# Attention's preparation: a stage of its own, or turned products and a side program within the first projection

## The chip, the cores and the metric

The kernel runs on one core of a Trainium2 chip. The time is that of the device in microseconds; lower is better. All data is float32 in memory.

## The reference

A chain of three layers over 1,024 latent and 256 context tokens of width 1,024: an attention layer, a recurrent layer (RWKV scan and a long convolution), and a block with gated mixing, a forgetting attention and a feed-forward net. The change concerns the first layer's input projection and what stands between it and the attentions:

```python
u = modulate(x, norm_g, shift, scale) @ w_in            # 1,280 tokens, 3,328 columns
qa, ka, va, ga, qb, kb, vb, gb = split_cols(u, (512, 512, 512, 512, 512, 128, 128, 512))
# local attention: qa (scaled), ka as they are
# grouped attention: 8 query and 2 key heads of 64
q_lat = apply_axial_rope(rms_norm(to_heads(qb, 8), q_gain), cos, sin)
k_lat = apply_axial_rope(rms_norm(to_heads(kb, 2), k_gain), cos, sin)
```

## The kernel before

The program is a sequence of stages. Each opens its own tiles and semaphores (`Stage`), writes one program for each engine, and ends by clearing its semaphores behind a barrier of all engines. Nothing is reordered: every engine runs its instructions as they are written, and semaphores order them against each other. All transfers named below are issued by SP.

`front_stage` makes the modulated tokens, turned, as a high and a low part (`xT`). `gemm_stage`, here named g1, then multiplies them with the weights: blocks of 416 columns, ten token tiles m of 128 in each block, eight steps k of 128, and three matmuls a step (high x high, high x low, low x high), so 24 matmuls for one product of 128 tokens and 416 columns. Each block of weights is loaded once (`w`) and split into a high part `wh` by ScalarE and a low part `wl` by VectorE, in four groups; both exist twice, so the next block's are made while this one's are used. There is a ring of five accumulators (`acc`) and five output tiles (`o`); VectorE evacuates even tiles m, ScalarE odd ones, and SP stores them into U1. VectorE's part of a split stands behind its second evacuation (m = 2), ScalarE's behind its second (m = 3). The sixth projection (named g6, 6 blocks of 428 columns, eight tiles) is a stage of the same kind.

`attn_prep_stage` follows g1. It reads U1 back and loops over five pairs of token tiles. For each pair, local attention's queries and keys (columns 0 to 1,023) are turned on TensorE (L508) and evacuated by ScalarE (L498), the queries scaled. The ten grouped heads (columns 2,048 to 2,687) are squared (ScalarE, L492), summed (VectorE, L523), a root taken (ScalarE, L494), scaled by its reciprocal and the gain (L526 to L529), rotated (L534 to L539), turned (TensorE, L514) and evacuated (VectorE). SP stores the 13 turned blocks into QT and waits for that store before the next pair. Ahead of the loop the stage zeroes three rows of U2. `na_stage` (local attention) and `gqa_stage` (grouped attention) read QT and U1.

The line on which the steps around a split rest, in VectorE's program of g1:

```python
for g in range(G):
    dve.wait_ge(high_out, (j * 2 + b) * G + g + 1)
    low(dve, wl[b][:, ks, :], w[:, ks, :], wh[b][:, ks, :]).then_inc(low_out, 1)
```

## Time and profile before

| | us |
|---|---|
| median of three runs | 5,387.6 |
| the runs | 5,382.7 to 5,405.49 |
| the profiled execution's own time | 5,381.02 |
| its span | 5,379.2 |
| mean granted TensorE clock | 0.895 |

The span runs from the first to the last instruction of one execution, which the hardware profiler recorded; start times count from its beginning. PE is TensorE's matmuls, PEld its weight loads, DVE VectorE, ACT ScalarE, POOL GpSimd, SP the queue that issues transfers. PEclk is the share of its full speed (2.4 GHz) that TensorE's clock was granted. In a timeline, what stands in brackets is how long the engine had been idle and what released it; rows merge instructions of one line (xcount), and a matmul's length there is its passage, longer than the spacing of one to the next.

### The profile page before, as it was taken

To read this page: it belongs to the slowest core of one execution; us is meant where nothing else is said; L and a number is where in the kernel's file an instruction comes from. 1 tells how busy PE (TensorE), PEld (TensorE's weight loads), DVE (VectorE), ACT (ScalarE), POOL (GpSimd) and SP (SyncE) were. 2 spreads that over 40 slices of the span, in tenths; PEclk is the share of its full clock that TensorE was granted. 3 is DMA by queue.
4 is the path that set the end of the run, shared out by engine and by line. 5 is a ranking of instruction groups with operands and counts; after the bars stand their busy time and mean duration, and the time that the engine had idled before them with its cause. 6 is when DMAs were issued, how large, how long until landed. Compare 5 with 4: busy or idle time off the path is not lost. (4 is left out here: it accounts for less than half of the span.)

```text
span 5379.2 us, 67544 instructions
## 1 busy us (share of the span) xinstructions
PE 4458.7 (83%) x25392; PEld 3788.9 (70%) x25392; DVE 2287.8 (43%) x4035; ACT 1508.8 (28%) x3230; POOL 889.5 (17%) x844
## 2 busy tenths in 40 slices
PE   8998279797888942899999968996793946899998
PEld 2898178797788931899999933445793735688876
DVE  3111467334511236667776754465311534211134
ACT  2110145465411124222222223004211534221133
POOL 0000053100000753444444432000000000000000
PEclk9999589898999976899998978998896967899999
DMA  7222352202322665211111141114222213111121
GB/s 281 89 84 69 119 111 51 55 16 77 114 88 100 222 217 209 71 37 36 45 44 30 31 133 47 74 39 150 83 86 75 57 56 110 63 47 50 35 86 67
DMA packets 295432, 464.36 MB, mean 86 GB/s; under 512 B 76576, under 2 KB 215936, under 8 KB 290629
## 3 DMA queue, kind: packets, MB, share of 16 engines
q1 hardware_dynamic: 294894, 455.99, 26.5%
q10 hardware_dynamic: 288, 5.07, 0.3%
q8 instruction: 152, 2.49, 0.2%
q14 instruction: 98, 0.80, 0.0%
HBM read 336.97 MB, written 129.01 MB: 87 GB/s over the span
## 5 line engine op out<-in xcount | busy, mean ns | idle before, releaser
L372 PE MATMUL g_acc<-g_wh,l_x_high 128*128 128x416 f32 (+2 forms) x1856 | 636.3, 343 | 58.0 <-DVE g_wl L53 58.0
L372 PE MATMUL g_acc<-g_wh,l_x_low 128*128 128x416 f32 (+2 forms) x1856 | 638.0, 344 | 0.0
L372 PE MATMUL g_acc<-g_wl,l_x_high 128*128 128x416 f32 (+2 forms) x1856 | 634.5, 342 | 0.0
L1480 POOL TENSOR_TENSOR scan_X<-scan_GA,scan_masks 64x256 f32<-64x256 f32 x480 | 361.9, 754 | 241.5 <-ACT scan_GA L1408 206.9
L372 PEld LDWEIGHTS g_acc<-g_wh,l_x_high 128*128 128x128 f32 x1856 | 351.7, 189 | 64.6 <-DVE g_wl L53 60.6
L428 DVE COPY g_o<-g_acc 128x416 f32<-128x416 f32 (+2 forms) x116 | 65.5, 565 | 715.3 <-PE g_acc L372 715.3
L372 PEld LDWEIGHTS g_acc<-g_wl,l_x_high 128*128 128x128 f32 x1856 | 352.2, 190 | 5.9
L3051 POOL TENSOR_TENSOR g_x<-g_x,g_o 128x512 f32<-128x512 f32 x8 | 11.1, 1396 | 2082.3 <-ACT g_o L2989 2082.2
L372 PEld LDWEIGHTS g_acc<-g_wh,l_x_low 128*128 128x128 f32 x1856 | 351.5, 189 | 3.6
L415 ACT COPY g_o<-g_acc 128x416 f32<-128x416 f32 (+2 forms) x116 | 56.5, 487 | 880.4 <-PE g_acc L372 880.4
L2835 PE MATMUL ffi_acc<-l4a_x_high,ffi_wh 128*128 128x512 f32 x704 | 274.7, 390 | 13.4 <-DVE ffi_wl L53 13.4
L2835 PE MATMUL ffi_acc<-l4a_x_low,ffi_wh 128*128 128x512 f32 x704 | 274.4, 390 | 0.0
L2835 PE MATMUL ffi_acc<-l4a_x_high,ffi_wl 128*128 128x512 f32 x704 | 274.3, 390 | 0.0
L1278 PE MATMUL scan_bank<-scan_T,scan_X 128*128 128x64 f32 x1600 | 211.0, 282 | 20.5 <-DVEq L1589 12.2
L53 DVE TENSOR_TENSOR ffi_wl<-ffi_w,ffi_wh 128x1024 fp32r<-128x1024 f32 x44 | 53.9, 1225 | 392.5 <-ACT ffi_wh L2845 392.5
L1278 PEld LDWEIGHTS scan_bank<-scan_T,scan_X 128*128 128x128 f32 x1600 | 196.1, 197 | 28.0 <-POOL scan_X L1480 26.6
L1286 PE MATMUL scan_bank<-scan_Pm,scan_TT 128*128 128x64 f32 x1600 | 201.9, 281 | 0.0
L1286 PEld LDWEIGHTS scan_bank<-scan_Pm,scan_TT 128*128 128x128 f32 x1600 | 194.7, 199 | 0.0
L1416 ACT COPY scan_Pm<-scan_bank 128x256 f32<-128x256 f32 x200 | 74.5, 373 | 392.1 <-PE scan_bank L1278 392.1
L1695 POOL TENSOR_TENSOR g_cu<-g_cu,g_ctaps 128x1536 f32<-128x1536 f32 x24 | 85.5, 3562 | 555.0 <-DMA g_cu<-s_U 555.0
L53 DVE TENSOR_TENSOR g_wl<-g_w,g_wh 128x832 fp32r<-128x832 f32 (+2 forms) x104 | 106.4, 1085 | 155.0 <-ACT g_wh L412 155.0
L2835 PEld LDWEIGHTS ffi_acc<-l4a_x_high,ffi_wh 128*128 128x128 f32 x704 | 132.5, 188 | 41.2 <-issue 13.7
(476 smaller groups left out, 9929.3 us busy)
## 6 DMA issues: line engine op xcount, KB each, us to landing
scan_F<-s_FE SPq DMA_DIRECT2D x160, 192.0 KB, 3.7
s_U<-g_o SPq DMA_DIRECT2D x120, 208.0 KB, 1.9
feat_u<-s_U SPq DMA_DIRECT2D x30, 832.0 KB, 11.1
s_FE<-feat_f SPq DMA_DIRECT2D x10, 2304.0 KB, 7.8
ffi_w<-in_w_ffn_in SPq DMA_DIRECT2D x44, 512.0 KB, 3.8
g_cu<-s_U SPq DMA_DIRECT2D x24, 768.0 KB, 5.1
g_w<-in_attn_w_in SPq DMA_DIRECT2D x8, 1664.0 KB, 7.1
pj_o<-s_O SPq DMA_DIRECT2D x26, 512.0 KB, 4.5
```

The lines of the kernel that those rows point to most:

```text
L53: return eng.tensor_tensor(to, src, hi.bitcast(F32), ALU.subtract)
L372: mm = pe.matmul(acc[r][:, 0:wn], xT[x][:, k, m * P:(m + 1) * P], v[b][:, k, :], start=(k == 0 and n == 0), stop=(k == kt - 1 and n == 2))
L415: nc.scalar.copy(o[m % R][:, :], acc[m % R][:, 0:wn]).then_inc(emptied[m % R], 1)
L428: dve.tensor_copy(o[m % R][:, :], acc[m % R][:, 0:wn]).then_inc(emptied[m % R], 1)
L1278: mm = pe.matmul(b[1][:, h * C:(h + 1) * C], X[d][:, l, h, :], T[d][:, h, :], start=True, stop=True)
L1286: mm = pe.matmul(b[1][:, 256 + h * C:256 + (h + 1) * C], TT[d][n % 2][:, h, :], Pm[d][:, h, :], start=True, stop=True)
L1416: nc.scalar.copy(flat(Pm[d][:, :, :]), b[1][:, 0:256]).then_inc(s["p_out"], 1)
L1480: pool.tensor_tensor(X[d][HALF[b], l, :, HALF[b]], GA[d][HALF[b], :, :], lev(d, l)[HALF[b], :].unsqueeze(1).to_broadcast([C, NP2, C]), ALU ...
L1695: link(pool.tensor_tensor(u[:, :, :], u[:, :, :], self.taps[c % 2][:, :, :], ALU.mult))
L2835: mm = pe.matmul(acc[b][2 * u + h][:, :], v[u][:, k, :], xT[x][:, k, h * 512:(h + 1) * 512], start=(k == 0 and n == 0), stop=(k == KT - 1 ...
L3051: pool.tensor_tensor(x[m][:, 0, :], x[m][:, 0, :], o[m][:, 0, :], ALU.add).then_inc(out_a, 1)
```

## The change

The preparation's stage goes. The first and the sixth projection become a stage written out in full, `products_stage`, over a list of blocks of chosen width and kind. Its products are numbered n over the whole stage. Block 0 and 1 (products 0 to 19) are the grouped queries and keys in two blocks of 384 columns. Then local attention's queries and keys come turned: the weights are the stationary side and the tokens the moving one, 512, 512 or 256 tokens a product, and the result goes straight into QT, the queries scaled on evacuation (blocks of 384, 384 and 256 columns: products 20 to 28, 29 to 37, 38 to 43). Then the rest as before, in blocks of 352, 336, 336, 256 and 256 columns (from product 44, 54, 64, 74 and 84; the last is 93). The next block's split stands behind the third or fourth product of a block: VectorE's behind the one with even n, ScalarE's behind the odd one. The first block of weights is loaded by four transfers.

`GroupedPrep` is a side program within this stage: for each of the ten token tiles t, its steps stand behind product 22 + 6t plus a phase: load at 0, square at 2, sum at 3, root at 4, scale at 5, rotate at 6, turn on TensorE at 7, evacuate at 8, store at 9 (each second tile). In the diff, lines of the removed stage are left out (they stand above), and so are declarations.

```diff
--- before.py
+++ after.py
...
-    pad, PADD, REP, table_in, table_out = table
+    PADD, REP, table_in, table_out = table
...
+def turned_block(w, c0, wn, spans, out_of, scale_of):
+    return dict(w=w[:, c0:c0 + wn].rearrange("(k p) n -> p k n", p=P), wn=wn,
+                items=[dict(turned=True, c=c, t0=t0, n=n, to=out_of(c0 + c * P, t0, n), scale=scale_of(c0 + c * P)) for c in range(wn // P) for t0, n in spans])
...
+def products_stage(nc, name, xT, kt, blocks, sides=()):
+    R, G = 5, 4
...
+                for g, ks in groups():
+                    sp.dma_start(w[:, ks, 0:blocks[0]["wn"]], blocks[0]["w"][:, ks, :]).then_inc(w0_in[g], 16)
+                for side in sides:
+                    side.begin(sp)
+                for n, (j, i, it) in enumerate(items):
+                    r = n % R
+                    sp.wait_ge(emptied[r], n // R + 1)
+                    sp.dma_start(it["to"], o[r][:, 0:it["n"]]).then_inc(stored[r], 16)
+                    if i == 0 and j + 1 < len(blocks):
+                        sp.wait_ge(low_out, G * (j + 1))
+                        sp.dma_start(w[:, :, 0:blocks[j + 1]["wn"]], blocks[j + 1]["w"]).then_inc(w_in, 16)
...
+                    for side in sides:
+                        side.transfers(sp, n, landed)
...
+                for n, (j, i, it) in enumerate(items):
+                    r, b = n % R, j % 2
+                    if n >= R:
+                        pe.wait_ge(emptied[r], n // R)
+                    for k in range(kt):
+                        if i == 0 and k % kg == 0:
+                            pe.wait_ge(low_out, j * G + k // kg + 1)
+                        for q, (x, v) in enumerate(((0, wh), (0, wl), (1, wh))):
+                            if it["turned"]:
+                                left, right = v[b][:, k, it["c"] * P:(it["c"] + 1) * P], xT[x][:, k, it["t0"]:it["t0"] + it["n"]]
+                            else:
+                                left, right = xT[x][:, k, it["m"] * P:(it["m"] + 1) * P], v[b][:, k, 0:it["n"]]
+                            mm = pe.matmul(acc[r][:, 0:it["n"]], left, right, start=(k == 0 and q == 0), stop=(k == kt - 1 and q == 2))
+                    mm.then_inc(summed[r], 1)
+                    for side in sides:
+                        side.products(pe, n)
...
+                    if i in (2, 3) and n % 2 and j + 1 < len(blocks):
+                        split(j + 1)
+                    for side in sides:
+                        side.scalars(act, n)
...
+                for n, (j, i, it) in enumerate(items):
+                    r = n % R
+                    if n % 2 == 0:
+                        dve.wait_ge(summed[r], n // R + 1)
+                        if n >= R:
+                            dve.wait_ge(stored[r], 16 * (n // R))
+                        if it["scale"] is None:
+                            dve.tensor_copy(o[r][:, 0:it["n"]], acc[r][:, 0:it["n"]]).then_inc(emptied[r], 1)
+                        else:
+                            dve.tensor_scalar(o[r][:, 0:it["n"]], acc[r][:, 0:it["n"]], it["scale"], None, ALU.mult).then_inc(emptied[r], 1)
+                    if i in (2, 3) and n % 2 == 0 and j + 1 < len(blocks):
+                        split(j + 1)
+                    for side in sides:
+                        side.vectors(dve, n)
...
+class GroupedPrep(Side):
...
+    NH, STRIDE = 10, 6
...
+    def at(self, n, phase):
+        t, d = divmod(n - self.first - phase, self.STRIDE)
+        return t if d == 0 and 0 <= t < self.NT else None
...
+    def transfers(self, sp, n, landed):
...
+        t = self.at(n, 0)
+        if t is not None:
+            if t == 0:
+                landed(sp, self.ready)
+            if t >= 2:
+                sp.wait_ge(self.roped, t - 1)
+            sp.dma_start(self.u[t % 2][:, :, :].rearrange("p h d -> p (h d)"), self.uv[t]).then_inc(self.u_in[t % 2], 16)
+            sp.dma_start(self.cs[t % 2][:, :, :], self.cv[t]).then_inc(self.u_in[t % 2], 16)
+        t = self.at(n, 9)
+        if t is not None and t % 2:
+            sp.wait_ge(self.evac_a, t + 1)
+            sp.wait_ge(self.evac_v, t + 1)
+            sp.dma_start(self.qv[t // 2], self.tb[t // 2 % 2][:, :, :]).then_inc(self.out[t // 2 % 2], 16)
...
+    def scalars(self, act, n):
+        t = self.at(n, 2)
+        if t is not None:
+            act.wait_ge(self.u_in[t % 2], 32 * (t // 2 + 1))
+            if t >= 2:
+                act.wait_ge(self.turned, 2 * (t - 1))
+            self.nc.scalar.activation(self.xn[t % 2][:, :, :], self.u[t % 2][:, :, :], ACT.Square).then_inc(self.squared, 1)
+        t = self.at(n, 4)
+        if t is not None:
+            act.wait_ge(self.ms_ready, t + 1)
+            self.nc.scalar.activation(self.ss[:, t % 2, :], self.ss[:, t % 2, :], ACT.Sqrt).then_inc(self.rt_ready, 1)
+        t = self.at(n, 8)
+        if t is not None:
+            act.wait_ge(self.turned, 2 * t + 1)
+            if t >= 4:
+                act.wait_ge(self.out[t // 2 % 2], 16 * (t // 4))
+            self.nc.scalar.copy(self.tb[t // 2 % 2][:, 0:4, t % 2 * P:(t % 2 + 1) * P],
+                                self.pt[0][:, :].rearrange("p (b t) -> p b t", t=P)).then_inc(self.evac_a, 1)
...
+        t = self.at(n, 3)
+        if t is not None:
+            xn, ss = self.xn[t % 2], self.ss[:, t % 2, :]
+            dve.wait_ge(self.squared, t + 1)
+            self.link(dve.tensor_reduce(ss, xn[:, :, :], AX.X, ALU.add))
+            dve.tensor_scalar(ss, ss, 1.0 / HD, NORM_EPS, ALU.mult, ALU.add).then_inc(self.ms_ready, 1)
+        t = self.at(n, 5)
+        if t is not None:
+            xn, ss = self.xn[t % 2], self.ss[:, t % 2, :]
+            dve.wait_ge(self.rt_ready, t + 1)
+            self.link(dve.reciprocal(ss, ss))
+            self.link(dve.tensor_tensor(xn[:, :, :], self.u[t % 2][:, :, :], ss.unsqueeze(2).to_broadcast([P, NH, HD]), ALU.mult))
+            dve.tensor_tensor(xn[:, :, :], xn[:, :, :], self.gain[:, :, :], ALU.mult).then_inc(self.scaled, 1)
+        t = self.at(n, 6)
+        if t is not None:
+            xn, cs, tmp = self.xn[t % 2], self.cs[t % 2], self.tmp
+            dve.wait_ge(self.scaled, t + 1)
+            for a in range(2):
+                for s in range(2):
+                    to, of = 32 * a + 16 * s, 32 * a + 16 * (1 - s)
+                    dve.tensor_tensor(tmp[:, :, to:to + 16], xn[:, :, of:of + 16], cs[:, 1:2, to:to + 16].to_broadcast([P, NH, 16]), ALU.mult).then_inc(self.seq, 1)
+                    self.link.n += 1
+            dve.wait_ge(self.seq, self.link.n)
+            self.link(dve.tensor_tensor(xn[:, :, :], xn[:, :, :], cs[:, 0:1, :].to_broadcast([P, NH, HD]), ALU.mult))
+            dve.tensor_tensor(xn[:, :, :], xn[:, :, :], tmp[:, :, :], ALU.add).then_inc(self.roped, 1)
+            dve.wait_ge(self.roped, t + 1)
+        t = self.at(n, 8)
+        if t is not None:
+            dve.wait_ge(self.turned, 2 * t + 2)
+            if t >= 4:
+                dve.wait_ge(self.out[t // 2 % 2], 16 * (t // 4))
+            dve.tensor_copy(self.tb[t // 2 % 2][:, 4, t % 2 * P:(t % 2 + 1) * P], self.pt[1][:, 0:P]).then_inc(self.evac_v, 1)
...
+    def products(self, pe, n):
+        t = self.at(n, 7)
+        if t is not None:
+            xf = self.xn[t % 2][:, :, :].rearrange("p h d -> p (h d)")
+            pe.wait_ge(self.roped, t + 1)
+            if t:
+                pe.wait_ge(self.evac_a, t)
+                pe.wait_ge(self.evac_v, t)
+            for k in range(5):
+                mm = pe.transpose(self.pt[k // 4][:, (k % 4) * P:(k % 4 + 1) * P], xf[:, k * P:(k + 1) * P], self.ident[:, :])
+                if k >= 3:
+                    mm.then_inc(self.turned, 1)
...
-                pad = s1.sb("pad", [HEADS, PADR, P])
                 table_in, table_out = s1.sem("table_in"), s1.sem("table_out")
-                front_stage(nc, ap, ident, gains, mods, x, ctx, xT, (pad, PADD, REP, table_in, table_out))
-                gemm(nc, "g1", xT, KT, LT + CT, ap["attn_w_in"][0], U1, 0, ATTN_IN, 416)
+                front_stage(nc, ap, ident, gains, mods, x, ctx, xT, (PADD, REP, table_in, table_out))
+                wa = ap["attn_w_in"][0]
+                def rows_of(c0, wn):
+                    return plain_block(wa, c0, wn, LT + CT, lambda m: U1[m * P:(m + 1) * P, c0:c0 + wn])
+                def turned_of(c0, wn):
+                    return turned_block(wa, c0, wn, ((0, 512), (512, 512), (1024, 256)), lambda c, t0, n: QT[c:c + P, t0:t0 + n],
+                                        lambda c: HD ** -0.5 if c < HW else None)
+                first = [rows_of(2048, 384), rows_of(2432, 384)]
+                rest = [turned_of(0, 384), turned_of(384, 384), turned_of(768, 256)]
+                rest += [rows_of(1024, 352), rows_of(1376, 336), rows_of(1712, 336), rows_of(2816, 256), rows_of(3072, 256)]
+                products_stage(nc, "g1", xT, KT, first + rest, [GroupedPrep(ap, ident, U1, QT, U2, 2 * (LT + CT), 2 * (LT + CT) + 2)])
                 with nc.Block() as block:
                     @block.sync
                     def _(sp):
                         sp.wait_ge(table_out, 16)
-            attn_prep_stage(nc, ap, ident, U1, QT, U2, (0, 5), 0, 0)
             na_stage(nc, ap, ident, U1, QT, REP, O1)
             gqa_stage(nc, ap, ident, U1, QT, O1)
             A2, B2, G2 = mods["rec"]
@@ -3127,7 +3333,8 @@
             project_stage(nc, "pj2", ident, LT, xT, lambda m: rows(O2)[m], ap["rec_w_out"][0], lambda m: rows(X1)[m],
                           lambda m: (gains[:, 0, :], None), gates_of=lambda h, m: gates2[h][m], gate_of=lambda m: G2[:, 0, :],
                           z_row=ap["final_norm"], z_out=lambda m: rows(H0)[m])
-            gemm(nc, "g6", xT, KT, LT, ap["w_in_2"][0], U3, 0, BLK_IN, 428)
+            products_stage(nc, "g6", xT, KT, [plain_block(ap["w_in_2"][0], c0, 428, LT, lambda m, c0=c0: U3[m * P:(m + 1) * P, c0:c0 + 428])
+                                              for c0 in range(0, BLK_IN, 428)])
         with Stage(nc, "l3a") as s3:
             csum = s3.sb("csum", [P, LT, HEADS])
             forget_stage(nc, ap, U3, csum)
```

How the order of instructions moves, at two places. VectorE, at a split: `g_wl` is the low part of the next weights, `g_o` an output tile, `g_p_` are tiles of the side program (`g_p_tmp` and L721, L722 the rotation, L722 signals `roped`). First before, in the loop over g1's blocks, where nothing but evacuations surround the split:

```order
L428 COPY g_o<-g_acc 128x416 [waits g1_stored2,g1_summed2]
L424 ISA
L53 TENSOR_TENSOR g_wl<-g_w,g_wh 128x832 [waits g1_high_out]
L424 REGISTER_ALU
L53 TENSOR_TENSOR g_wl<-g_w,g_wh 128x832 [waits g1_high_out]
L424 REGISTER_ALU
L53 TENSOR_TENSOR g_wl<-g_w,g_wh 128x832 [waits g1_high_out]
L424 REGISTER_ALU
L53 TENSOR_TENSOR g_wl<-g_w,g_wh 128x832 [waits g1_high_out]
L428 COPY g_o<-g_acc 128x416 [waits g1_stored4,g1_summed4]
```

After, at products 46 to 48:

```order
L562 COPY g_o<-g_acc 128x352 [waits g1_stored1,g1_summed1]
L53 TENSOR_TENSOR g_wl<-g_w,g_wh 128x2x336 [waits g1_high_out] x4
L718 TENSOR_TENSOR g_p_tmp<-g_p_xn,g_p_cs 128x10x16 [waits g1_p_scaled]
L718 TENSOR_TENSOR g_p_tmp<-g_p_xn,g_p_cs 128x10x16 x3
L721 TENSOR_TENSOR g_p_xn<-g_p_xn,g_p_cs 128x640 [waits g1_p_seq]
L722 TENSOR_TENSOR g_p_xn<-g_p_xn,g_p_tmp 128x640 [waits g1_p_seq]
L562 COPY g_o<-g_acc 128x352 [waits g1_stored3,g1_summed3,g1_p_roped]
L729 COPY g_p_tb<-g_p_pt 128x128 [waits g1_p_turned]
```

The rotation of tile 3 now stands behind the split's four low parts, and these wait for ScalarE's `high_out`.

TensorE, at the turns (`ident` is the identity, `pt` what is turned into). Before, a pair's turns stand in the preparation's own loop:

```order
L508 MATMUL prep_pt<-main_ident,prep_u 128x128 [waits prep0_loaded0]
L508 MATMUL prep_pt<-main_ident,prep_u 128x128 x7
L508 MATMUL prep_pt<-main_ident,prep_u 128x128 [waits prep0_loaded1]
L508 MATMUL prep_pt<-main_ident,prep_u 128x128 x7
L514 MATMUL prep_pt<-main_ident,prep_xn 128x128 [waits prep0_roped]
L514 MATMUL prep_pt<-main_ident,prep_xn 128x128 x4
L514 MATMUL prep_pt<-main_ident,prep_xn 128x128 [waits prep0_roped]
L514 MATMUL prep_pt<-main_ident,prep_xn 128x128 x4
```

After, those of tile 3 stand within the products, behind product 47:

```order
L514 MATMUL g_acc<-g_wh,l_x_low 128x352
L740 MATMUL g_p_pt<-main_ident,g_p_xn 128x128 [waits g1_p_evac_v,g1_p_evac_a,g1_p_roped]
L740 MATMUL g_p_pt<-main_ident,g_p_xn 128x128 x4
L514 MATMUL g_acc<-g_wh,l_x_high 128x352 [waits g1_emptied3]
L514 MATMUL g_acc<-g_wl,l_x_high 128x352
```

The next product stands behind the turns, and these wait for `roped`; turns of local queries and keys (L508) are no longer there.

## Rows read from the trace of the kernel before

**Rows 1.** The page's head and TensorE's busy time; columns: us, share, instructions.
```profile
span 5379.2 us, 67544 instructions
...
PE 4458.7 (83%) x25392; PEld 3788.9 (70%) x25392; DVE 2287.8 (43%) x4035; ACT 1508.8 (28%) x3230; POOL 889.5 (17%) x844
```

**Rows 2.** Engines by stretch: us; PE, PEld, DVE, ACT, POOL; PEclk, DMA share, GB/s.
```profile
500.00:600.00 100.00, 37.88 (x178) 33.35 (x177) 33.99 (x69) 10.90 (x22) 0.00 (x0) 0.61 0.31 101
600.00:700.00 100.00, 20.93 (x84) 16.42 (x83) 36.59 (x72) 13.62 (x27) 15.84 (x10) 0.50 0.56 148
```

**Rows 3.** Timeline: last product, preparation's first transfer, next stage's first transfer.
```profile
519.59 0.35 PE L372 MATMUL g_acc<-g_wh,l_x_low 128*128 128x416 f32 x1
...
525.39 0.34 SPq L456 DMA_DIRECT2D prep_gq<-in_gqa_q_gain  x1
...
673.06 1.21 SPq L646 DMA_DIRECT2D na_q_raw<-s_QT  x2
```

**Rows 4.** Timeline: one token tile of the preparation, start us and us.
```profile
532.36 0.33 SPq L479 DMA_DIRECT2D prep_cs<-in_rope  x1
...
536.09 0.74 ACT L492 ACTIVATE prep_sq<-prep_u 128x640 f32<-128x640 f32 x1 [15.60 <-DMA prep_cs<-in_rope]
...
538.16 0.22 DVE L526 RECIPROCAL prep_ss<-prep_ss 128x10 f32<-128x10 f32 x1 [0.28 <-ACT prep_ss L494]
...
540.13 1.03 DVE L534 TENSOR_TENSOR prep_tmp<-prep_xn,prep_cs 128x160 f32<-128x160 f32 x4
...
542.94 1.33 PE L514 MATMUL prep_pt<-main_ident,prep_xn 128*128 128x128 f32 x5 [1.20 <-DVE prep_xn L539]
```

**Rows 5.** Products alone by stretch: 416, 320 and 512 columns wide, in this order.
```profile
160.00:500.00 340.00, 340.00 (x1801) 336.85 (x1800) 1.00 0.24 82
1600.00:1700.00 100.00, 100.00 (x684) 100.00 (x683) 1.00 0.26 85
...
4700.00:4800.00 100.00, 100.00 (x443) 82.81 (x442) 1.00 0.17 51
```

**Rows 6.** Timeline of TensorE in local attention: 256-column products, then turns.
```profile
893.03 0.28 PE L735 MATMUL na_scores<-na_k_low,na_q_two 128*128 128x256 f32 x1
893.15 0.34 PE L734 MATMUL na_scores<-na_k_high,na_q_two 128*128 128x384 f32 x1
...
895.00 0.93 PE L751 MATMUL na_pt<-main_ident,na_prob 128*128 128x128 f32 x7
895.69 0.36 PE L734 MATMUL na_scores<-na_k_high,na_q_two 128*128 128x256 f32 x1
```

**Rows 7.** Timeline of ScalarE, then VectorE, at one split in the first projection.
```profile
220.78 0.51 ACT L415 COPY g_o<-g_acc 128x416 f32<-128x416 f32 x1 [8.48 <-PE g_acc L372]
...
222.11 3.83 DVE L53 TENSOR_TENSOR g_wl<-g_w,g_wh 128x832 fp32r<-128x832 f32 x4 [5.27 <-ACT g_wh L412]
225.86 0.58 DVE L428 COPY g_o<-g_acc 128x416 f32<-128x416 f32 x1
```

**Rows 8.** Products of the fourth projection's first 12 us by stretch, after 14.19 us idle.
```profile
1738.00:1744.00 6.00, 5.94 (x17) 5.69 (x18) 0.50 0.41 156
1744.00:1750.00 6.00, 6.00 (x33) 5.93 (x33) 0.99 0.46 120
```

**Rows 9.** The granted clock (PEclk) around two idle times, and those times.
```profile
3798.00:3800.00 2.00, 0.00 (x0) 0.00 (x0) 0.54 (x2) 1.23 (x3) 0.00 (x0) 0.73 0.01 4
...
3805.51 1.94 PE L2579 MATMUL pj_pn<-main_ident,pj_t 128*128 128x128 f32 x8 [8.77 <-ACT pj_t L2652]
...
915.00:920.00 5.00, 4.25 (x37) 4.26 (x38) 4.28 (x10) 3.09 (x7) 0.00 (x0) 1.00 0.00 0
...
915.75 0.98 PE L751 MATMUL na_pt<-main_ident,na_prob 128*128 128x128 f32 x7 [2.13 <-ACT na_prob L799]
```

**Rows 10.** Timeline: first weight load of the first projection, and its first use.
```profile
145.49 0.38 SPq L326 DMA_DIRECT2D g_w<-in_attn_w_in  x1
152.26 2.46 ACT L412 CAST g_wh<-g_w 128x832 fp32r<-128x832 f32 x3 [25.37 <-DMA g_w<-in_attn_w_in]
```

More of the change, by code:

```diff
@@ L100, in front_stage @@
         xs = [st.sb(f"x{m}", [P, D]) for m in range(NT)]
+        pad = st.sb("pad", [HEADS, PADR, P])
         given = st.sb("given", [P, P])
@@ new lines, in products_stage, with _, open, begin @@
+            pools = [side for side in sides if side.on_pool]
+            if pools:
+                @block.gpsimd
+                def _(pool):
+                    for side in pools:
+                        side.pools(pool)
+class Side:
+    on_pool = False
+    def open(self, nc, st):
+        self.nc = nc
+    def begin(self, sp):
+        return None
+    def transfers(self, sp, n, landed):
+        return None
+    def products(self, pe, n):
+        return None
+    def scalars(self, act, n):
+        return None
+    def vectors(self, dve, n):
+        return None
+    def end(self, sp):
+        return None
```

205 lines of the change are left out of this document (104 added, 101 removed).

## The prediction

> **What bounds the kernel now.** The page's head comes first: one core, TensorE busy for 83% of 5,379.2 us [rows 1], so what counts is where TensorE stands. The table by stretch shows such a place: from 500 to 700 us it is busy for 38% and 21%, with no other engine above 37% and the granted clock at 0.61 and 0.50 [rows 2]. That is the preparation. It runs as ten tiles in five rounds, each a chain of a transfer, ScalarE, VectorE and turns on TensorE with a barrier behind it, so latency bounds it. Its first transfer issues at 525.39, the next stage's first at 673.06, and TensorE's last product before it began at 519.59 [rows 3]. The first projection itself is bound by TensorE, 340.00 busy of 340 us with 1,801 products: 0.1888 us each, 0.1883 at the steadiest [rows 5]; VectorE and ScalarE have slack there, and one split shows it: VectorE had stood 5.27 us waiting for ScalarE's high parts [rows 7].
>
> **What is removed.** The stage as a whole: 673.06 - 525.39 = 147.7 us [rows 3]. What precedes it after the last product (evacuation, store, clearing, barrier: 525.39 - 519.94 = 5.5 us) stays, now ahead of local attention. That stage clears 20 more semaphores; no row prices one, so nothing to 2 us, taken 1.0.
>
> **Products.** Spacings: 320 columns 100/684 = 0.1462, 416 columns 0.1883, 512 columns 100/443 = 0.2257 [rows 5], and 256 columns 893.15 - 893.03 = 0.120 [rows 6]. Between 320 and 416 I interpolate: 0.153 for 336, 0.160 for 352, 0.174 for 384. Before, 80 products of 24 matmuls: 1,920 x 0.1883 = 361.5 us. Now 94: 480 x 0.174 (the grouped columns), 384 x 0.2257 + 192 x 0.120 (turned), 240 x 0.160, 480 x 0.153 and 480 x 0.120 make 363.2. So +1.7: the 512-wide products pay for the narrow ones. The 80 turns of local queries and keys are gone and cost nothing elsewhere, since the products come out turned. The written-out program costs nothing extra as far as rows 6 show, for attention is written out too and issues every 0.12 us.
>
> **Side program, its own time on TensorE.** Ten times five turns. Seven turns take 895.69 - 895.00 = 0.69 us at the full clock [rows 6], so five take 0.5, with 0.1 for the change of shape: 6.0 us. Bounds: 5, and 11 with all of it at the half clock, where five turns before a drain took 1.33 [rows 4].
>
> **Side program, what TensorE waits for.** TensorE turns tile t behind product 29 + 6t, and stands in order until VectorE has rotated it. VectorE rotates behind product 28 + 6t, after evacuating it. The rotation is 542.94 - 540.13 = 2.81 us, and the scaling ahead of it 540.13 - 538.16 = 1.97 [rows 4]. Usually the next product covers evacuation and rotation: 24 x 0.153 = 3.7 us against 0.5 + 2.8, a margin of 0.4. Not where a split of the next weights stands between them. VectorE's split falls on the even one of a block's third and fourth products, ScalarE's on the odd one; where the even one is first, VectorE stands until the later product is summed. Rotations follow products 28, 34, ..., 82; splits follow 2, 12, 22, 32, 40, 46, 56, 66, 76. They meet at 40, 46 and 76, and the turns that need the rotation follow 41, 47 and 77, the very products that ScalarE's split waits for. So each stall is, from the end of the odd product: evacuation and first cast (1.33 us for 416 columns: 222.11 - 220.78), four low parts (3.83 us for 832 elements, scaled by width) and the rotation [rows 4, 7].
> Product 41 (352 columns come next): 1.3 + 3.2 + 2.8 = 7.3.
> Product 47 (336 next): 1.1 + 3.1 + 2.8 = 7.0.
> Product 77 (256 next): 0.9 + 2.4 + 2.8 = 6.1.
> At 56 the split meets the scaling of tile 5: 4.2 + 2.0 + 0.5 + 2.8 = 9.5 against two products, 7.4: 2.1. At 82 there is no split, but the 256-wide product covers 2.9 of 3.3: 0.4.
> Together 23.0 us. Behind each waiting turn all later products queue; ScalarE, SP and the stores then wait for these in turn and add nothing. The ring of five accumulators has been emptied by then. Tile loads are hidden: ScalarE squares a tile two products behind its load, 5.8 us or more, and the last of a tile's transfers was used 3.7 us after its issue (536.09 - 532.36) [rows 4]; tile 7's load is issued just behind a weight load and may come some us late, but its turns are seven products off.
>
> **The clock.** TensorE stood idle for 8.77 us before 3805.51, so from 3796.7, and over 3798 to 3800 its clock averaged 0.73, on its way from 1.00 to 0.50; a gap of 2.13 left it at 1.00 [rows 9]. So the three long stalls end at the half clock (1.2 GHz), the short ones not. A restart showed 17 products in 6 us and then 33 in 6 us [rows 8]: 16 x 0.188 = 3.0 us lost. Three of them: 9.0; bounds 0 and, with five, 15.
>
> **The first weight load** is now four transfers, and each quarter is used when it lands. Before, 1,664 KB were used 152.26 - 145.49 = 6.8 us after issue [rows 10]. A quarter is about the size of one prepared tile's loads, and these were used 3.7 us after the last issue [rows 4], so TensorE starts 3.1 us sooner; cold products (6 x 0.32 = 1.9 us a quarter) are slower than the quarters arrive. The sixth projection gets the same: -6.2, bounds 0 and -8.
> The Trainium skill ("SBUF — State Buffer", The DMA setup-cost knee) speaks against splitting: a transfer pays some 2 us whatever its size, so the largest single transfer is best. Taken one after the other, four would by its formula (2 us and 436 GB/s) land 11.6 us after issue and be split at 13.4, where TensorE would ask for the last quarter at 3.7 + 2.0 + 3 x 1.9 = 11.4: 2 us later at each of the two places, 5,278 for the whole, an estimate. This trace has six loads issued some 0.5 us apart of which the first tile's three were all there 3.7 us after the third's issue, so I take them as overlapping.
>
> **Sum:** -147.7 + 1.0 + 1.7 + 6.0 + 23.0 + 9.0 - 6.2 = -113.2. It is made against the profiled execution, 5,381.0 us, 6.6 below the median of 5,387.6; on the median it gives 5,274.4. A measurement of this kernel can tell about 0.5%, 27 us, from no change.
>
> **Rivals.**
> 1. The stalls don't come, as VectorE's split finds the high parts ready or TensorE has slack: 5,274.4 - 23.0 - 9.0 = 5,242. For it speaks only that engines other than TensorE are mostly idle; against it the written order and VectorE's 5.27 us wait [rows 7]. 0.12.
> 2. The side program stops TensorE at nearly every tile: the margin of 0.4 us in the 336-wide blocks is within semaphore delays and slower VectorE work. Five more stalls of 2 us, with the clock falling at each (3.0), make +25, and +6 for cold turns: 5,305. 0.13.
> 3. It ends slower: written out, 2,256 and 1,152 products (first and sixth projection) are fed to TensorE more slowly than the loops were. It needs 113 + 27 = 140 us over 3,408 products, 41 ns each; at 50 ns (0.238 instead of 0.188) the kernel takes 5,445. Written-out attention at 0.120 us speaks against it [rows 6]. 0.03.
> 4. The preparation's latency is paid inside instead: the whole chain of a tile (532.36 to 542.94, 10.6 us) stands on TensorE ten times, plus ten restarts of 3.0, 136 us in place of 32: 5,378, no change. It needs a tile's steps to be late by all of the seven products that lie between its load and its turns, some 27 us at 3.8 each. 0.02.
> The forecast has 0.70.
>
> **How the numbers follow.** The likeliest is 5,274. The range reaches down to rival 1 and up to just short of rival 2, which adding the upper bounds of turns, clock and first load (5 + 6 + 6) to 5,274 nearly gives too: 5,242 to 5,300. Rivals 3 and 4 and most of 2 are left out. Faster: 0.70 + 0.12 + 0.13 = 0.95; same 0.02; slower 0.03.
>
> **What would show it.** In the profile after: no preparation stage; the first projection from its first product to its last about 363 + 6 + 23 + 9 + 3 for the cold start = 404 us; TensorE's waits for the rotated tile (line 722) three long ones of 6 to 7.5 us and one of 2, and nowhere else; clock at half behind these three; 512-wide turned products at 0.226 and 256-wide at 0.120; the first cast 3 us sooner after its load's issue. The prediction is wrong if the waits stand at other tiles, if the narrow products keep the spacing of the wide ones (weight loads would then bound them), or if local attention's first transfer comes much more than 6 us behind the last product.

## The result, and the profile after

The changed kernel takes 5,238.8 us (median; 5,234.5 to 5,255.6), the kernel before in the same job 5,385.2 (5,379.3 to 5,405.5): a ratio of 0.9725 [0.9697, 0.9752]. Faster, as forecast, but by 146 us where 113 were forecast, and 3 us under the range's low end of 5,242. The profiled execution lasts 5,236.3 us against 5,379.2 before [rows 1]. Of the 76 executions of the kernel before that all jobs of this document have beside the others, one, at 6,269.9 us and a mean clock of 0.709, is slow and stands in no comparison.

The page's head of the changed kernel; columns as in [rows 1]:
```profile
span 5236.3 us, 67314 instructions
...
PE 4412.2 (84%) x25648; PEld 3739.7 (71%) x25648; DVE 2284.1 (44%) x4040; ACT 1508.1 (29%) x3235; POOL 888.2 (17%) x844
```
Its timeline at the first weight load, at the end of the first projection and at local attention's first transfer, to be held against [rows 3, 10]:
```profile
146.34 1.92 SPq L484 DMA_DIRECT2D g_w<-in_attn_w_in  x4
...
149.76 0.83 ACT L528 CAST g_wh<-g_w 128x768 fp32r<-128x768 f32 x1 [22.02 <-DMA g_w<-in_attn_w_in]
...
151.64 0.69 PE L514 MATMUL g_acc<-g_wh,l_x_high 128*128 128x384 f32 x1 [9.87 <-DVE g_wl L53]
...
152.99 0.83 ACT L528 CAST g_wh<-g_w 128x768 fp32r<-128x768 f32 x1 [0.28 <-DMA g_w<-in_attn_w_in]
...
552.29 0.28 PE L514 MATMUL g_acc<-g_wh,l_x_low 128*128 128x256 f32 x1
...
558.41 1.17 SPq L842 DMA_DIRECT2D na_q_raw<-s_QT  x2
```
No stage stands between the projection and local attention, whose first transfer moves from 673.06 [rows 3] to 558.41: -114.65 us. From the first product to the last it is 400.7 us (forecast 404), and 5.8 us lie between the last product and that transfer.

TensorE's waits for the rotated tile up to there; columns: engine, tile and line, what it waited for, us in total, times, longest. Then the timeline of the turns that had to wait:
```profile
PE g_p_pt L740 <- DVE g_p_xn L722: 22.8, 5, 7.3
```
```profile
347.06 1.33 PE L740 MATMUL g_p_pt<-main_ident,g_p_xn 128*128 128x128 f32 x5 [7.34 <-DVE g_p_xn L722]
...
381.23 1.33 PE L740 MATMUL g_p_pt<-main_ident,g_p_xn 128*128 128x128 f32 x5 [7.05 <-DVE g_p_xn L722]
...
432.21 0.76 PE L740 MATMUL g_p_pt<-main_ident,g_p_xn 128*128 128x128 f32 x5 [1.94 <-DVE g_p_xn L722]
...
503.30 1.33 PE L740 MATMUL g_p_pt<-main_ident,g_p_xn 128*128 128x128 f32 x5 [6.17 <-DVE g_p_xn L722]
...
523.00 0.77 PE L740 MATMUL g_p_pt<-main_ident,g_p_xn 128*128 128x128 f32 x5 [0.30 <-DVE g_p_xn L722]
```
The five stalls are the five of the prediction. Behind the three long ones five turns take 1.33 us, in the other seven tiles 0.71 to 0.77. The clock had fallen to half behind the long ones, as the first two rows and the last show; each covers 12 us from just behind a turn, and the row at 424 holds the stall of 1.94 us:
```profile
348.00:360.00 12.00, 12.00 (x59) 10.48 (x58) 1.79 (x4) 1.07 (x3) 0.00 (x0) 0.80 0.07 24
382.00:394.00 12.00, 12.00 (x63) 12.00 (x62) 1.62 (x4) 1.15 (x3) 0.00 (x0) 0.80 0.08 25
...
424.00:436.00 12.00, 10.06 (x67) 9.79 (x67) 7.94 (x14) 3.66 (x7) 0.00 (x0) 1.00 0.26 76
...
504.00:516.00 12.00, 12.00 (x93) 12.00 (x93) 3.35 (x8) 1.07 (x3) 0.00 (x0) 0.90 0.10 34
```

So the changed stage came out near the forecast. The other 28 us lie behind it, and all but some 3 of them where nothing was changed. By the first transfer of each stage the program is 114.65 us ahead at local attention, 119.6 when the scan starts (at 2,160.4 before, at 2,040.8 after), 141.4 when the scan ends (3,132.8 and 2,991.4) and 142.9 at the end. The scan runs the same instructions in 972.4 us before and in 950.6 now. Engines by stretch over the whole scan, columns as in [rows 2], before with three pieces of it, and then after:
```profile
2160.40:3132.80 972.40, 934.38 (x7840) 919.94 (x7840) 689.54 (x1491) 252.88 (x713) 408.80 (x582) 0.96 0.16 39
2836.00:2846.00 10.00, 8.65 (x75) 8.30 (x74) 8.83 (x19) 1.34 (x4) 9.10 (x13) 1.00 0.01 2
2846.00:2856.00 10.00, 10.00 (x48) 9.64 (x47) 4.07 (x9) 1.53 (x6) 4.82 (x7) 0.53 0.00 0
2856.00:2896.00 40.00, 40.00 (x193) 39.64 (x192) 16.78 (x39) 8.36 (x23) 1.93 (x4) 0.52 0.19 47
```
```profile
2040.80:2991.40 950.60, 914.02 (x7840) 900.00 (x7840) 688.96 (x1492) 253.10 (x713) 408.44 (x582) 0.98 0.16 40
...
2726.00:2736.00 10.00, 10.00 (x83) 9.85 (x84) 6.63 (x13) 2.06 (x7) 6.32 (x9) 1.00 0.09 24
2736.00:2776.00 40.00, 39.01 (x341) 38.40 (x341) 32.59 (x72) 11.41 (x32) 18.67 (x27) 1.00 0.18 42
```
Before, TensorE issues 193 products in 40 us at a granted clock of 0.52 and is busy for all of them; after, 341 at 1.00. The clock stood at half (1.2 GHz) for some 48 us, from 2,846.6 to 2,894.4, with no idle time of TensorE ahead of it but two waits of under 1 us. I call such a stretch, with TensorE busy and no long wait ahead of it, a fall. One costs 972.4 - 950.6 = 21.8 us.

### The profile page after: what moved, and what is told of

Same layout as the page of the kernel before. It is cut to its first block and busy times, and to the rows that moved or that the text cites. A ratio compares the mean times of both kernels' runs of the same rounds, so it can differ in the third digit from the quotient of the medians.

```text
span 5236.3 us, 67314 instructions
## 1 busy us (share of the span) xinstructions
PE 4412.2 (84%) x25648; PEld 3739.7 (71%) x25648; DVE 2284.1 (44%) x4040; ACT 1508.1 (29%) x3235; POOL 888.2 (17%) x844
## 5 line engine op out<-in xcount | busy, mean ns | idle before, releaser
L514 PE MATMUL g_acc<-g_wh,l_x_high 128*128 128x428 f32 (+4 forms) x944 | 315.9, 335 | 22.3 <-DVE g_wl L53 22.3
L514 PE MATMUL g_acc<-g_wh,l_x_low 128*128 128x428 f32 (+4 forms) x944 | 314.8, 333 | 0.0
L514 PE MATMUL g_acc<-g_wl,l_x_high 128*128 128x428 f32 (+4 forms) x944 | 314.8, 333 | 0.0
L373 PE MATMUL g_acc<-g_wh,l_x_high 128*128 128x320 f32 (+1 forms) x832 | 273.5, 329 | 29.3 <-DVE g_wl L53 29.3
L373 PE MATMUL g_acc<-g_wl,l_x_high 128*128 128x320 f32 (+1 forms) x832 | 272.5, 328 | 0.0
L373 PE MATMUL g_acc<-g_wh,l_x_low 128*128 128x320 f32 (+1 forms) x832 | 271.0, 326 | 0.0
L1474 PEld LDWEIGHTS scan_bank<-scan_T,scan_X 128*128 128x128 f32 x1600 | 191.2, 192 | 26.9 <-POOL scan_X L1676 25.4
L514 PEld LDWEIGHTS g_acc<-g_wh,l_x_high 128*128 128x128 f32 x944 | 180.6, 191 | 27.2 <-DVE g_wl L53 24.3
L562 DVE COPY g_o<-g_acc 128x428 f32<-128x428 f32 (+5 forms) x65 | 35.6, 548 | 368.1 <-PE g_acc L514 367.9
L514 PEld LDWEIGHTS g_acc<-g_wl,l_x_high 128*128 128x128 f32 x944 | 180.7, 191 | 2.8
L514 PEld LDWEIGHTS g_acc<-g_wh,l_x_low 128*128 128x128 f32 x944 | 180.1, 191 | 2.4
L373 PEld LDWEIGHTS g_acc<-g_wh,l_x_high 128*128 128x128 f32 x832 | 157.7, 190 | 30.6 <-DVE g_wl L53 30.0
```

The costliest lines, as they stand in the source:

```text
L373: mm = pe.matmul(acc[r][:, 0:wn], xT[x][:, k, m * P:(m + 1) * P], v[b][:, k, :], start=(k == 0 and n == 0), stop=(k == kt - 1 and n == 2))
L514: mm = pe.matmul(acc[r][:, 0:it["n"]], left, right, start=(k == 0 and q == 0), stop=(k == kt - 1 and q == 2))
L562: dve.tensor_copy(o[r][:, 0:it["n"]], acc[r][:, 0:it["n"]]).then_inc(emptied[r], 1)
L1474: mm = pe.matmul(b[1][:, h * C:(h + 1) * C], X[d][:, l, h, :], T[d][:, h, :], start=True, stop=True)
```

## The experiments

The theories. **One**: the changed stages give -113 to -121, and the rest is a fall in the scan that the kernel before has and the changed one mostly does not have. **Two**: the changed kernel speeds the scan itself, or the first projection gave more than its rows show. Beside them, the terms of the sum are tried one at a time.

### The same two programs again
No edit.

> The kernel before, unchanged, profiled a second time. In the first profile of it TensorE's granted clock stood at 0.50 from about 2,846.5 to 2,894.4 us, in the middle of the scan stage, while TensorE was busy; the changed kernel's profile has no such stretch in its scan, and 22.5 of its 142.9 us lie there. Theory one, the fall belongs to this program (its executions repeat it at the same place): the fall is there again at about 2,846, the profiled execution takes 5,381 us and the scan stage (first transfer to the last product) as long as before. Theory two, it is chance in each execution: the fall is elsewhere or absent, the profiled time about 5,357 without it, and the runs of this kernel scatter by 20 us.

Measured: 5,382.2 us (5,372.6 to 5,404.4), ratio 0.9995 [0.9971, 1.0019]; its record has one fall, 686 us into the scan as in the first record, and a scan of 972.3.

> The changed kernel, unchanged, for more runs of it: 29 runs of the kernel before were never under 5,372, so all had the fall in the scan; of four of the changed kernel three lay at 5,235 to 5,239 and one at 5,256. Theory one, whether the fall comes is chance in each execution and the changed program meets it less often: the runs lie in two groups, near 5,237 and 20 us higher, the lower one the larger. Theory two, the changed program never meets it: nearly all runs near 5,237.

Measured: 5,238.5, ratio 0.969 [0.9659, 0.9722]; five of six executions lie at 5,236 to 5,242, one at 5,264, and the record has no fall (scan 951.0). Both kernels repeat, and the time comes in steps of 20 to 28 us: those of before stood at 5,375 to 5,386 and at 5,400 to 5,411 in one job (15 and 8). No execution of before in any job lay below 5,372, where one without a fall belongs (5,360).

### The side program ahead of the split
```
                     for side in sides:
                         side.vectors(dve, n)
                     if i in (2, 3) and n % 2 == 0 and j + 1 < len(blocks):
                         split(j + 1)
```


> The changed kernel with the two calls in VectorE's program of the products exchanged: the side program's steps stand ahead of the split, so the rotations behind products 40, 46 and 76 no longer wait for the high parts of the next weights. By the prediction's step the three long stalls (7.3, 7.0 and 6.1 us) go with their three clock falls (9.0), the one of 2.1 behind product 59 and the one of 0.4 behind 83 stay: the first projection 29 us shorter, the whole about 5,239 - 29 = 5,210. Rival: the stalls come from somewhere else (a transfer, ScalarE's root), then TensorE's waits for the rotated tile stay at 22.8 us and the time is 5,239. If the scan's clock falls in this program, either figure is 22 us higher, and the profile shows it.

> The changed kernel with the side program's vectors ahead of the split, once more and in more executions. Two groups of times are expected 8 to 11 us or 20 us and more apart, as in its first four (5,230.2 and 5,230.4; 5,239.7 and 5,240.4, the upper with one fall of the clock inside the scan in its record). If the fall in the scan is what kept its first run from the 5,210 forecast, the executions without a fall should stand near 5,217 (profiled span 5,238.4 less 21.5) and a profile without one should have a scan of 951 us. If there is no execution under 5,225, the fall is bound to this kernel's order and is not chance. The transfer of na's first tile should again start near 533 us.

Measured: first 5,235.0 us, ratio 0.9702 [0.9652, 0.9751]; again 5,220.1, 0.9692 [0.9665, 0.9719]. VectorE now rotates before it turns to the split. The chain of waits in the first run:
```profile
PE g_p_pt L740 <- DVE g_p_xn L722: 2.5, 3, 1.9
```
The stalls went from 22.8 us to 2.5, and local attention's first transfer stands at 533.4 and 531.5, 25.0 and 26.9 us sooner (forecast 29: 20.3 of stalls, the rest restarts of the clock). In the first run's record the scan took it back: one fall, 972.2 us. In the second it has none, 951.2, and the span is 5,207.8. The executions of the second: 5,207.9, 5,209.9, 5,211.2 and 5,229.0, 5,232.5, 5,233.7. So the stalls were worth what they lasted and the restarts behind them. One fall hides nearly all of it, and from a few executions alone the edit would have looked worthless. Only three of its ten executions in both runs are without a fall (5,208 to 5,211); the median of all ten is 5,230, that of the changed kernel's ten 5,239.

### The preparation of grouped attention as its own stage
The turned products stay. Edit in the program:
```
-            ... rest, [GroupedPrep(ap, ident, U1, QT, U2, 2 * (LT + CT), 2 * (LT + CT) + 2)])
+            ... rest)
+            attn_prep_stage(nc, ap, ident, U1, QT, U2, (0, 5), 0, 0)   # grouped columns only
             na_stage(nc, ap, ident, U1, QT, REP, O1)
```


> Only one part of the change: the products as in the changed kernel (local queries and keys computed turned, written out), but the grouped preparation as a stage of its own with the loop over five pairs as before, now without the local turns, without their loads and with a store of 5 blocks instead of 13. By the prediction's account what bounds the old stage is the chain of load, VectorE's two tiles and the store with its barrier, and the local turns lay beside it: the stage stays about 130 to 145 us of the 147.7 long, the first projection is 38 us shorter than in the changed kernel (no stalls, no falls, no grouped turns), so the whole is 5,239 + 137 - 38 = about 5,338. Rival: the local turns and their transfers were what made the old stage long; then the stage falls to 80 to 100 us and the whole is about 5,290.

Measured: 5,338.2, ratio 0.9888 [0.9836, 0.9941]; local attention's first transfer at 645.19, 86.8 us later than in the changed kernel (99 by the forecast). The stage lasts 123.8 us (521.37 to 645.19), a little less than the 130 to 145 expected and far more than the rival's 80 to 100. Its windows show the same picture as [rows 2]:
```profile
560.00:640.00 80.00, 10.63 (x40) 7.43 (x40) 46.51 (x94) 5.56 (x13) 0.00 (x0) 0.50 0.18 54
```
TensorE is busy for 13% at half clock. Of the 115 us about a quarter comes from turned queries and keys and three quarters from moving the grouped part inside, though the stage kept less than half of its turns. So the stage's time is mostly its chain, not its work: without the local turns and their transfers it lost 23.9 of its 147.7 us.

### One load for the first weights
```
-                for g, ks in groups():
-                    sp.dma_start(w[:, ks, ...], blocks[0]["w"][:, ks, :]).then_inc(w0_in[g], 16)
+                sp.dma_start(w[:, :, ...], blocks[0]["w"]).then_inc(w0_in[0], 16)
```


> The changed kernel with the first block of weights of both rewritten projections loaded by one transfer again instead of four. By the prediction's step each start comes 3.1 us later, the whole 6 us slower, 5,245; the changed kernel's first cast began 3.4 us after its load's issue, the kernel before's 6.8. By the page's rule that a transfer pays its 2 us whatever its size, taken one after the other, it would be 4 us less than that, so 2 us slower than the changed kernel. The profile tells: time from the load's issue to the first cast and from there to the 25th product.

Measured: 5,254.7, ratio 0.9704 [0.9664, 0.9744], two executions at 5,242 and 5,246 and two at 5,264 and 5,265. Its timeline at both places:
```profile
146.38 0.38 SPq L483 DMA_DIRECT2D g_w<-in_attn_w_in  x1
153.04 3.03 ACT L527 CAST g_wh<-g_w 128x768 fp32r<-128x768 f32 x4 [25.12 <-DMA g_w<-in_attn_w_in]
...
154.92 0.69 PE L513 MATMUL g_acc<-g_wh,l_x_high 128*128 128x384 f32 x1 [13.11 <-DVE g_wl L53]
...
3694.43 0.39 SPq L483 DMA_DIRECT2D g_w<-in_w_in  x1
3701.46 3.33 ACT L527 CAST g_wh<-g_w 128x856 fp32r<-128x856 f32 x4 [11.85 <-DMA g_w<-in_w_in]
3703.51 0.72 PE L513 MATMUL g_acc<-g_wh,l_x_high 128*128 128x428 f32 x1 [16.11 <-DVE g_wl L53]
```
From issue to first product 8.5 us and 9.1 against 5.3 and 5.4 with four transfers: 3.2 and 3.7 us (forecast 3.1 each). The Trainium skill ("SBUF — State Buffer", The DMA setup-cost knee) counts some 2 us for each transfer whatever its size, and advises one transfer as large as possible where transfers bound the time. By the estimate from its figures, with the four taken one after the other, this edit would have cost 2 us over both places. The traces do not agree: it cost 6.9. With four transfers, issued 0.5 us apart, ScalarE starts on the fourth quarter 6.65 us behind the first issue (146.34 to 152.99), just when it starts on the whole block with one transfer (146.38 to 153.04, 6.66). So the four overlapped, and the first user needs only the first.

### A wait ahead of the scan
Transfers of 16 columns, each waited for, in a stage of their own:
```
+        with Stage(nc, "idle") as sd:
+            ...
+                    for k in range(4):      # 8 in before_idle8
+                        sp.dma_start(dot[:, :], ap["ident"][:, 0:16]).then_inc(landed, 16)
+                        sp.wait_ge(landed, 16 * (k + 1))
         rwkv_scan_stage(nc, ap, ident, FE, YS)
```


> The kernel before with an idle stage ahead of the scan: four transfers of 8 KB, each waited for, some 15 us with the stage's own barrier. Nothing else changes. Theory one of the scan's clock (it falls at a fixed place of this program): the fall comes at the same step of the scan, some 15 us later, and the time is 5,385 + 15 = 5,400. Theory three (what decides is at which moment, counted from something outside the scan, its steps arrive): the fall moves to another step or vanishes, and the time is 5,400 or, without it, 5,377.

> The changed kernel with the same idle stage ahead of the scan, which cost the kernel before 7.1 us and took the fall from 4 of its 10 runs. Theory one, how often the fall comes hangs on when the scan starts against something that is not in the program: the idle stage changes the share here too, and some of the runs, where the changed kernel has nearly none, show it: two groups, near 5,244 and near 5,266. Theory two, the removed preparation itself is what keeps the fall away: all runs near 5,244.

> The same kernel with the idle stage of four transfers, each waited for, ahead of the scan; it costs 7.1 us, as before_idle and after_idle showed. If the point at which the scan starts decides whether the clock falls inside it, the scan now starts 7.1 us later against whatever the clock goes by and the share of executions with a fall should change from swap's: executions without one near 5,224, with one near 5,246. If the fall does not depend on the start, the share is swap's own and the median is 7 us over swap's.

> The kernel before with an idle stage of eight such transfers (about 14.2 us) ahead of the scan. Four of them took the fall away in 4 of 10 executions (5,361.5 to 5,369.8). If the start of the scan decides, the share should be another again with eight: all of them with a fall would give 5,382 + 14 = 5,396, none 5,374. If four transfers helped only by leaving TensorE idle longer, eight should help at least as often: 5,374 in half of the executions or more.

Measured: the four transfers cost 7.1 us in the record, not 15 (first transfer of the features to that of the scan 238.7 us against 231.6), eight 13.1 (244.7). before_idle: 5,382.1, ratio 0.9965 [0.9935, 0.9995]; four of ten executions at 5,361.5 to 5,369.8, the others 5,378.6 to 5,392.9. The record is of a low one, and where before had its fall, from 686 us into the scan, it has none:
```profile
2852.00:2892.00 40.00, 39.80 (x349) 39.35 (x349) 30.36 (x66) 12.34 (x35) 15.88 (x23) 1.00 0.20 47
```
Its scan takes 951.2 us: the kernel before, none of its work changed, can run the short scan, and the first record of swap, whose scan is also unchanged, has the long one. For the scan that settles theory one against two. after_idle: 5,267.3, ratio 0.973 [0.9698, 0.9762]; two of six at 5,245 to 5,247, four at 5,265 to 5,274. swap_idle: 5,216.7, ratio 0.9682 [0.9656, 0.9707]; five of six at 5,214 to 5,222, and the record is of the sixth (5,242.8, one fall, a scan of 972.5). before_idle8: 5,394.5, ratio 1.0001 [0.9985, 1.0017]; one of twelve at 5,377.3, eleven at 5,388 to 5,399.

Executions without a fall, by their times:

| | no idle stage | four transfers | eight |
|---|---|---|---|
| before | 0 of 85 | 4 of 10 | 1 of 12 |
| changed | 8 of 10 | 2 of 6 | not run |
| swap | 3 of 10 | 5 of 6 | not run |

So the share moves when the scan starts some us later, in no direction that I can name. The groups are small: only the 4 of 10 against none of 85 are clear, and the other shares could differ by chance. The place moves too: in the seven records with one fall it begins 374 to 774 us into the scan.

### Spare products
```
# before_warm: in level_p, ahead of the waits of level 2 in emitting chunks
+                        if l == 2 and n and emits(n - 1):
+                            for x in range(3):
+                                pe.matmul(bank[0][3][:, 256:384], ident[:, :], ident[:, :], ...)
# before_start: ahead of the scan's first sums, 110 of the same
```


> The kernel before with three spare products (identity times identity, into a part of an accumulator that is free there) ahead of each of the two waits of the scan's second level, in the chunks that also form outputs. In four profiles with a clock fall in the scan (both of the kernel before, the one with the calls exchanged, the one with the preparation apart) it came right behind these two waits of 0.35 and 0.44 to 0.79 us, at different chunks, and held the half clock for 47.8 us. Theory one, the fall is TensorE's clock answering to the thin activity at this step: with the waits filled it is gone, the scan takes about 950 instead of 972 us and the whole about 5,362, with all its runs below 5,375 but for other falls. Theory two, the fall has nothing to do with this step: it comes as often as before, the runs stay at 5,375 to 5,387 and the profile shows it in the scan.

> The kernel before with 110 spare products of 128 columns on TensorE at the start of the scan, in the 30 us in which it waits for the scan's first load (nothing of the result uses them). The clock then stands at full when the scan's own first products come, where it now stands at half for 17 to 20 us from the first load: that alone should give 5 to 8 us back, 5,375 to 5,380. If the fall inside the scan hangs on the state in which the scan starts, the scan's time should become the short one (951 less those 5 to 8) and the whole 5,350 to 5,358; if not, one fall stays and the scan is 964 to 967 us.

Measured: before_warm 5,402.9, ratio 0.9997 [0.9969, 1.0026]. The kernel before stood high in that job: five executions near 5,380, six near 5,404 and five near 5,428. The record of before_warm has three falls, where theory one wanted none, and a scan of 1,000.5 us:
```profile
2626.00:2660.00 34.00, 34.00 (x159) 33.64 (x159) 14.14 (x34) 4.33 (x15) 1.85 (x4) 0.50 0.23 54
2816.00:2850.00 34.00, 34.00 (x175) 33.54 (x174) 15.26 (x37) 5.08 (x17) 5.54 (x9) 0.57 0.23 55
3006.00:3050.00 44.00, 44.00 (x244) 43.54 (x243) 20.75 (x47) 7.63 (x24) 9.61 (x15) 0.61 0.18 43
```
The short waits were filled and the falls came all the same, so these waits do not bring them. before_start: 5,426.9, ratio 1.006 [1.0038, 1.0082]. Here I misread the cover: the 30 us of idle time end 7 us behind the scan's first transfer, and the spare products (26.9 us, from 2,165.6) held the first real ones up to 2,192.3, 30.2 us behind that transfer where it had been 6.8. So they cost 23 us there, of which the full clock gave some 3 back. The times come at 5,403 to 5,406 (five), 5,426 to 5,432 (six) and 5,454 (one), 20 to 28 us apart; the record has two falls, in a scan of 1,014.5 us. A full clock at the start takes no fall away, though here the scan's products also start later.

### Waits inside the scan
```
# SyncE, chunk n (every fourth, or every one)
+                    sp.wait_ge(e[1]["dt_mm"], 5 * n + 5)
+                    sp.dma_start(dot[:, :], ap["ident"][:, 0:16]).then_inc(gap, 16)
# TensorE, ahead of mix_w(n - 1)
+                        pe.wait_ge(gap, ...)
```


> The kernel before; in chunks 4, 8, 12 and 16 of the scan TensorE waits at the chunk's end for one small transfer that is issued only when its last product is through, some 2.3 us each, about 9 us in all. If long unbroken activity of TensorE brings the fall (spare products in the scan's waits gave three falls, none taken away gave one or two), some executions should be without one: 5,361 + 9 = 5,370. If it hangs on the point at which the scan starts, which is unchanged, every execution keeps one or two: 5,391 and 5,413.

> The same in each of the 16 emitting chunks, about 37 us of waits in all. If unbroken activity brings the fall, there should be none in any execution and the scan should take 951 + 37 = 988 us, the whole 5,398. If the start decides, one or two falls stay: 5,420 and 5,442. Waits that the scan's other engines use to run ahead would make each cheaper than 2.3 us.

Measured: 5,443.2, ratio 1.0076 [1.0043, 1.011], and 5,542.6, 1.0275 [1.0227, 1.0324]. The four waits of before_gap4 last 1.6, 5.3, 5.2 and 5.2 us, 4.3 in the mean and not 2.3. The first of them in the timeline:
```profile
2420.39 0.69 PE L1303 MATMUL scan_bank<-scan_S,scan_AR 128*128 128x64 f32 x2 [1.59 <-DMA scan_dot<-in_ident]
```
Windows of before_gap4: 10 us behind three of the four waits, a fall, the scan:
```profile
2424.00:2434.00 10.00, 10.00 (x66) 10.00 (x66) 3.17 (x7) 5.82 (x14) 0.00 (x0) 0.69 0.00 0
2797.00:2807.00 10.00, 10.00 (x55) 10.00 (x55) 1.39 (x3) 3.66 (x10) 0.00 (x0) 0.56 0.01 2
3007.00:3017.00 10.00, 10.00 (x49) 10.00 (x49) 0.63 (x1) 2.98 (x8) 0.00 (x0) 0.50 0.01 2
2870.00:2918.00 48.00, 48.00 (x222) 47.28 (x222) 19.50 (x45) 8.31 (x25) 6.70 (x11) 0.51 0.16 39
...
2157.70:3167.40 1009.70, 955.39 (x7840) 940.38 (x7840) 689.93 (x1491) 253.40 (x713) 409.52 (x582) 0.93 0.16 37
```
Behind each wait the clock stands at half for some 10 us, behind the one of 1.59 us too (until 2,430). So one wait costs (1,009.7 - 972.3) / 4 = 9.4 us, more than twice its length; in before_gap1 sixteen, 4.5 us in the mean, cost 1,128.3 - 972.3 = 156 us, 9.8 each. The fall of 48 us is still there, between the waits. In before_gap1 one of 36 us (2,942 to 2,978) begins 31 us behind a wait that ended at 2,911.3 and is over before the next ends at 2,981.8. So long unbroken activity isn't what brings it either.

## Why the prediction was right and wrong

**Right, term by term.** The stage is gone and what preceded it stayed (5.8 us against 5.5). The stalls were to be 7.3, 7.0, 2.1, 6.1 and 0.4 and are 7.34, 7.05, 1.94, 6.17 and 0.30 us: 22.8 for 23.0. They came out of the written order of two programs (which of the two products a split falls on) and three durations. Half clock stood behind the three long ones and not behind the short, though before_gap4 shows that a wait as short as 1.59 us can have it behind it, so it was in part luck that the short stalls left the clock alone. The restarts were priced at 9.0 from an idle time of 14 us; by windows of 1 us the half clock ends 5.7, 5.7 and 3.1 us behind the start of the turns, and half of that is 7.2 us lost. The first product comes 3.2 to 3.7 us sooner behind its load (3.1). The sixth projection's stage went from 240.1 us to 237.3 (-3.1 forecast). To local attention's first transfer the sum gives -110.1 (without that 3.1) and -114.65 came, 4.5 us more. The restarts make 1.8 of these; some 1.5 more is an estimate from the start of the projection, where the half clock lasted 3 us behind the first product (151.64 to 154.7) and had lasted 6 before (154.26 to 160.2). The 1.0 us for clearing semaphores has no row behind it, and 0.3 came (5.8 against 5.5). Two sums are off by little: the products' terms as written make 362.7 and not 363.2, the stalls 22.9 and not 23.0.

**Rivals.** Rival 1's 5,242 is close to the time, and its mechanism did not happen: the stalls came, at full size. It was near by its number alone. Nothing of rival 2 (no wait at a sixth tile, no more than five), rival 3 (256-column products stand 0.12 us apart, 546.17 to 546.29) or rival 4 is in the profile. The estimate by the Trainium skill's figures is answered by one_load: the four transfers did not go one after the other.

**The step that failed** is the last: "It is made against the profiled execution, 5,381.0 us". The sum priced the changed stages and took all behind them as they stood in that one execution. That execution held a fall in the scan, worth 21.8 us, which eight of the changed kernel's ten executions lack. By stretch of the two records: -114.65 up to local attention (forecast -110.1), -4.9 from there to the scan (forecast nothing), -21.8 in the scan (nothing), -1.5 behind it (forecast -3.1), together -142.9. The -4.9 is no gain either: from local attention to the scan the same instructions took between 1,478.2 and 1,487.9 us in the twelve records without an idle stage there. Without the fall it is -121.1, 5,266 from the median before: 8 us from the forecast and inside its range. Two rows in the scan would have shown it beforehand, one with 44 to 49 products in 10 us and one with 83 to 94, both fully busy: the prediction read no window there, since nothing was changed. It would still not have told how often the changed kernel falls; but it would have named a case at 5,250 with a chance, and carried the range to 5,230.

**What is shown and what is not.** Shown: the fall, its price (21 to 23 us between scans with none and with one, in twelve records: 950.6 to 951.2 in five of them, 972.0 to 973.0 in seven), that the kernel before runs without it too, and that it masks an edit of 25 us. That the groups of times are numbers of falls is argued from these steps; each record fits its group. Open: what brings it. It is not the two short waits ahead of it, not a half clock at the scan's start, and not long unbroken activity. It depends on the timing ahead of the scan, for 7 us of waiting took it from four of ten executions of before, where it had come in all 85. That the changed kernel is mostly spared is then no merit of its edits. Of the 142.9 us between the two records the edited stages show 114.65 + 2.8, some 117.

## To carry to other kernels

Before the sum is set against a measured time, look through the clock row of the whole program, the unchanged stages too: a stretch with TensorE fully busy and half as many products as its neighbours is time that a shift alone can give back or take. Where a side program shares an in-order engine with the main one, list which of its steps meets which of the main one's in the written order; here the stalls came out to within 0.2 us, and the cure (the short, awaited work ahead of the long) is worth their length and the restarts of the clock behind them, here 25 to 27 us. Compare executions with the same number of falls: the best version measured is swap, 5,208 to 5,211 us without one, against 5,235 to 5,242 for the changed kernel.

## What the hardware showed that was not expected

The granted clock fell to half while TensorE was busy for all of a stretch, for 34 to 48 us, once to three times in a scan of a millisecond; the same program had it in some executions and not in others, and whole executions lie in groups 20 to 28 us apart. Four waits of 4.3 us in the mean inside a busy stretch cost 9.4 us each, since each, the one of 1.59 us too, was followed by some 10 us of half clock; the stall of 1.94 us in the changed kernel was not.
